# The first weight piece of two mixtures in four parts, and products nobody reads ahead of two waits of each router

## The reference

```python
def grouped_moe(h, router_w, router_b, w_gate, w_up, w_down):
    scores = jax.nn.sigmoid(t @ router_w)                # 16 experts
    sel = scores + router_b
    # best of 4 groups by the sum of its two best experts, then two experts in that group
    combine = ...                                        # (tokens, 16), mostly zero
    for e in range(N_EXPERTS):
        he = jax.nn.silu(t @ w_gate[e]) * (t @ w_up[e])
        y = y + combine[:, e:e + 1] * (he @ w_down[e])

def first_block(x, c, ...):
    for layer in range(2):
        mod = (silu(c) @ ada_w[layer] + ada_b[layer])    # six rows: shifts, scales, gates
        h = rms_norm(x, norm1_g[layer]) * (1.0 + sc1) + sh1
        x = x + g1 * (even_mixer(h, ...) if layer == 0 else odd_mixer(h, ...))
        h = rms_norm(x, norm2_g[layer]) * (1.0 + sc2) + sh2
        x = x + g2 * grouped_moe(h, ...)

def second_block(x, mem, ...):                           # after it, two more layers:
    # feed-forward, rwkv7 or dilated attention, each beside attention to mem, feed-forward
```

## Time and profile before

| | us |
|---|---|
| time, median of 3 runs | 2259.53 (2258.82 to 2261.78) |
| time of the profiled execution | 2259.21 |
| its span | 2257.4 |
| PE busy | 2159.8 (96%) |
| DVE busy | 1408.3 (62%) |
| ACT busy | 1030.3 (46%) |

### The profile page before, as it was taken

The page is one execution under the profiler, slowest core; times in us unless marked ns, Lnnn a source line. Parts: engine busy times, 40 slices in busy tenths (PEclk is TensorE's granted clock), DMA queues, the critical chain, the costliest instruction groups (busy, mean ns, idle before and its releaser), DMA issues.

```text
span 2257.4 us, 32929 instructions
## 1 busy us (share of the span) xinstructions
PE 2159.8 (96%) x14046; PEld 1774.0 (79%) x14046; DVE 1408.3 (62%) x1456; ACT 1030.3 (46%) x1155; POOL 80.8 (4%) x138
## 2 busy tenths in 40 slices
PE   6998899999999899999999999889999999999999
PEld 4777777678787777678788897778888888888887
DVE  5776745689775743499756555466566576635654
ACT  4344422367545423277544445335444444435443
POOL 2040000000000000000000000000000000020000
PEclk9999899999999899999999999999999999999999
DMA  9872869999670858999555550005554555433553
GB/s 345 308 250 96 305 244 368 367 345 368 207 255 1 282 188 314 333 339 364 196 188 186 186 168 18 4 34 197 198 187 167 184 182 203 146 88 126 192 186 112
DMA packets 267313, 475.61 MB, mean 211 GB/s; under 512 B 9424, under 2 KB 151824, under 8 KB 262944
## 3 DMA queue, kind: packets, MB, share of 16 engines
q1 hardware_dynamic: 256128, 431.81, 55.0%
q0 software_dynamic: 11040, 41.70, 5.4%
HBM read 471.33 MB, written 2.14 MB: 210 GB/s over the span
## 4 chain that ended last, share of the span: by engine, by line
PE 86%; DVE 6%; ACT 4%; DMA 2%; issue 1%; POOL 0%; ACTq 0%; DVEq 0%; SPq 0%; POOLq 0%
PE psum L1074 14%; PE psum L1076 7%; PE psum L1091 3%; PE psum L1093 3%; PE psum L1092 3%; PE psum L1042 3%; PE psum L1044 3%; PE psum L1043 3%; PE psum L1411 3%; PE psum L1366 2%; PE psum L1367 2%; PE psum L1368 2%; PE psum L1523 2%; PE psum L1525 2%; PE psum L1524 2%; DVE w_lo L2806 2%
## 5 line engine op out<-in xcount | busy, mean ns | idle before, releaser
L2806 DVE TENSOR_TENSOR w_lo<-ring,w_hi 128x2048 fp32r<-128x2048 f32 x267 | 609.9, 2289 | 288.3 <-ACT w_hi L2157 282.1
L2157 ACT ACTIVATE w_hi<-ring 128x2048 fp32r<-128x2048 f32 x267 | 510.8, 1915 | 367.9 <-PE psum L1093 119.8
L1074 PE MATMUL psum<-h_both,w_hi 128*128 128x512 f32 x1408 | 499.4, 399 | 1.6 <-DVE h_both L3500 1.3
L1076 PE MATMUL psum<-h_both,w_lo 128*128 128x256 f32 x1408 | 395.3, 281 | 0.0
L1074 PEld LDWEIGHTS psum<-h_both,w_hi 128*128 128x128 f32 x1408 | 264.5, 188 | 68.0 <-issue 1.7
L1076 PEld LDWEIGHTS psum<-h_both,w_lo 128*128 128x128 f32 x1408 | 265.9, 189 | 1.4
L2806 DVE TENSOR_TENSOR w_lo<-pool,w_hi 128x2048 fp32r<-128x2048 f32 x70 | 160.4, 2292 | 103.7 <-ACT w_hi L2157 103.3
L2157 ACT ACTIVATE w_hi<-pool 128x2048 fp32r<-128x2048 f32 x70 | 134.1, 1916 | 161.5 <-DMA pool<-in_exp_w_up 58.9
L2179 ACT ACTIVATE pool<-psum 128x512 f32<-128x512 f32 x88 | 52.6, 598 | 261.1 <-PE psum L1076 261.1
L1042 PE MATMUL psum<-w_hi,h_both 128*128 128x512 f32 (+1 forms) x352 | 142.1, 404 | 5.7 <-DVE w_lo L2806 2.7
L1366 PE MATMUL psum<-h_both,w_hi 128*128 128x256 f32 x480 | 139.1, 290 | 0.2 <-DVE w_lo L2806 0.2
(11 more groups left out here) (476 smaller groups left out, 3795.6 us busy)
## 6 DMA issues: line engine op xcount, KB each, us to landing
ring<-in_ffn_pre_w_in SPq DMA_DIRECT2D x44, 1024.0 KB, 5.1
ring<-in_ffn_post_w_in SPq DMA_DIRECT2D x44, 1024.0 KB, 5.1
pool<-in_exp_w_up SPq DMA_DIRECT2D x40, 1024.0 KB, 7.9
ring<-in_exp_w_gate SPq DMA_DIRECT2D x36, 1024.0 KB, 7.6
ring<-in_exp_w_down SPq DMA_DIRECT2D x30, 1024.0 KB, 7.6
ring<-in_ada_w SPq DMA_DIRECT2D x24, 1024.0 KB, 7.0
ring<-in_ffn_pre_w_out SPq DMA_DIRECT2D x22, 1024.0 KB, 4.8
ring<-in_ffn_post_w_out SPq DMA_DIRECT2D x22, 1024.0 KB, 4.9
```

Source lines behind the costliest of these rows:

```text
L1074: pe.matmul(o.rearrange("p (s n) -> p s n", s=2), wh[:, k, fs], h_both[:, :, k, :], start=k == 0, stop=False, skip_group_check=True)
L1076: m = pe.matmul(o[:, 0:T], wl[:, k, fs], h_hi[:, k, :], start=False, stop=k == KD - 1, skip_group_check=True)
L2157: act.activation(w_hi[:, (s["split"] + r) % 3, :], piece(s["pieces"][r]), ACT.Copy)\
L2806: dve.tensor_tensor(w_lo[:, slot, :], piece(s["pieces"][r]), w_hi[:, slot, :].bitcast(F32), ALU.subtract).then_inc(sem("w_lo"), 1)
```

## The change

First, the first piece of each mixture is loaded in four parts of 256 columns by two blocks, cast in four parts, and multiplied in high parts in four steps; DVE makes its low part in two halves. Second, the broadcast of the experts' weights is split: its first half stays in the router, its second stands behind the second quarter of the first piece; the copies of it move from the router into the mixture on ACT and DVE. Third, PE makes 5 (layer 0) or 10 (layer 1) unread products ahead of its wait for `group_picked` and 7 ahead of its wait for `comb_tok`. Fourth, the new semaphores `part_in0` to `part_in3` take the places of others: `mem_w01`, `cols_in` and `hot_in` become one, `tables_in`, and each wait for one of them becomes a wait for all ten loads (160); `rotated` and the first three quarters share `rotated_parts_hi`; `rwkv_in` and `stored` are counted on `landed0`.

```diff
+TABLES = 160
...
+                self.add(kind, (name, c, half), ("w_lo", self.split), slot, 0 if n == 0 else 1)
...
+                    elif n == m["first"]:
+                        src, dst = expert(kind, layer, 4 * group[0], 0), piece(n).rearrange("p (k n) -> p k n", k=KD)
+                        for j in range(4):
+                            sp.dma_start(dst[:, 2 * j:2 * j + 2, :], src[:, 2 * j:2 * j + 2, :]).then_inc(sem(f"part_in{j}"), 16)
...
-                pl.dma_start(mem_w[layer][half], src).then_inc(sem("mem_w1" if layer else f"mem_w0{half}"), 16)
+                pl.dma_start(mem_w[layer][half], src).then_inc(sem("mem_w1" if layer else ("tables_in" if half else "mem_w0")), 16)
...
-            pl.dma_start(rcols[:, :], a["rwkv_cols"]).then_inc(sem("cols_in"), 16)
+            pl.dma_start(rcols[:, :], a["rwkv_cols"]).then_inc(sem("tables_in"), 16)
             pl.dma_start(gains64[:, :, :], a["gains64"].partition_broadcast(P).rearrange("p (n d) -> p n d", d=64))\
-              .then_inc(sem("cols_in"), 16)
-            pl.dma_start(router_b[:, :], a["router_b"].partition_broadcast(P)).then_inc(sem("cols_in"), 16)
-            pl.dma_start(router_w[:, :, :], a["router_w"].rearrange("(k p) n -> p k n", p=P)).then_inc(sem("cols_in"), 16)
...
+              .then_inc(sem("tables_in"), 16)
+            pl.dma_start(router_b[:, :], a["router_b"].partition_broadcast(P)).then_inc(sem("tables_in"), 16)
+            pl.dma_start(router_w[:, :, :], a["router_w"].rearrange("(k p) n -> p k n", p=P)).then_inc(sem("tables_in"), 16)
...
-            pl.dma_start(view(WORK + 4240, 12)[0:32, :], a["rel_bias_2"]).then_inc(sem("hot_in"), 16)
...
+            pl.dma_start(view(WORK + 4240, 12)[0:32, :], a["rel_bias_2"]).then_inc(sem("tables_in"), 16)
...
-                    pe.wait_ge(sem("cols_in"), 64)
-                    pe.wait_ge(sem("hot_in"), 80)
+                    pe.wait_ge(sem("tables_in"), TABLES)
...
-            pe.wait_ge(sem("mem_w01"), 16)
+            pe.wait_ge(sem("tables_in"), TABLES)
             mem_products(0, 4)
             pe.wait_ge(sem("ada_used"), KD)
...
+                warm(10 if layer else 5, 2)
                 pe.wait_ge(sem("group_picked"), layer + 1)
                 picked = rt[:, 392:400]
                 pe.matmul(bank(6)[:, 0:8], K["ones"], picked, start=True, stop=True).then_inc(sem("group_sums"), 1)
                 pe.matmul(bank(7)[:, 0:8], K["ones"], picked, start=True, stop=False)
                 pe.matmul(bank(7)[:, 0:8], K["neg_from"], picked, start=False, stop=True).then_inc(sem("group_sums"), 1)
+                warm(7, 2)
                 pe.wait_ge(sem("comb_tok"), layer + 1)
                 for t in range(NT):
                     m = pe.transpose(bank(5)[0:NE, P * t:P * t + P], comb_tok[:, NE * t:NE * t + NE], ident)
                 m.then_inc(sem("comb_T_ps"), 1)
                 pe.wait_ge(sem("comb_T"), layer + 1)
                 pe.wait_ge(sem("places_in"), layer + 1)
-                for e in range(4):
-                    m = pe.matmul(bank(6 + e // 2)[:, T * (e % 2):T * (e % 2) + T],
-                                  bc(ident[0:NE, e:e + 1], [NE, P]), comb_t, start=True, stop=True)
-                    if e % 2:
-                        m.then_inc(sem("comb_ps"), 1)
+                comb_rows(0)
+
+            def comb_rows(half):
+
+                for e in range(2):
+                    m = pe.matmul(bank(6 + half)[:, T * e:T * e + T], bc(ident[0:NE, 2 * half + e:2 * half + e + 1], [NE, P]), comb_t,
+                                  start=True, stop=True)
+                m.then_inc(sem("comb_ps"), 1)
 
...
                     n = at[kind, c, 0]
-                    if n == 0:
-                        pe.wait_ge(sem("w_split_hi"), U0 + 1)
-                    else:
+                    if n > 0:
                         pe.wait_ge(sem("w_lo"), U0 + n + 1)
                     pe.wait_ge(sem("silu_done" if kind == "gate" else "hid_ready"), G0 + c + 1)
                     wh, wl = halves(n, HC)
                     if n == 0:
-                        for f in range(2):
-                            for k in range(KD):
-                                o, fs = bank(4)[:, T * f:T * f + T], slice(P * f, P * f + P)
-                                pe.matmul(o, wh[:, k, fs], h_hi[:, k, :], start=k == 0 and f == 0, stop=False, skip_group_check=True)
-                                pe.matmul(o, wh[:, k, fs], h_lo[:, k, :], start=False, stop=False, skip_group_check=True)
+                        for j in range(4):
+                            if j < 3:
+                                pe.wait_ge(sem("rotated_parts_hi"), 1 + 3 * layer + j + 1)
+                            else:
+                                pe.wait_ge(sem("w_split_hi"), U0 + 1)
+                            for k in (2 * j, 2 * j + 1):
+                                for f in range(2):
+                                    o, fs = bank(4)[:, T * f:T * f + T], slice(P * f, P * f + P)
+                                    pe.matmul(o, wh[:, k, fs], h_hi[:, k, :], start=k == 0 and f == 0, stop=False, skip_group_check=True)
+                                    pe.matmul(o, wh[:, k, fs], h_lo[:, k, :], start=False, stop=False, skip_group_check=True)
+                            if j == 1:
+                                comb_rows(1)
                         pe.wait_ge(sem("w_lo"), U0 + 1)
...
-            pe.wait_ge(sem("rwkv_in"), 96)
+            pe.wait_ge(sem("landed0"), PL.rwkv_landed)
...
-            act.wait_ge(sem("cols_in"), 64)
+            act.wait_ge(sem("tables_in"), TABLES)
             split_piece("even_in", 0, 0)
...
-                act.wait_ge(sem("comb_ps"), 2 * layer + 1)
-                act.activation(flat(comb_b[:, 0:2, :]), bank(6), ACT.Copy).then_inc(sem("side_act"), 1)
...
-                for n in range(3):
+                act.wait_ge(sem("w_used"), U0 - 2)
+                for j in range(4):
+                    cols = slice(512 * j, 512 * j + 512)
+                    act.wait_ge(sem(f"part_in{j}"), 16 + 16 * layer)
+                    act.activation(w_hi[:, U0 % 3, cols], piece(m_["first"])[:, cols], ACT.Copy)\
+                       .then_inc(sem("rotated_parts_hi" if j < 3 else "w_split_hi"), 1)
+                    if j == 1:
+                        act.wait_ge(sem("comb_ps"), 2 * layer + 1)
+                        act.activation(flat(comb_b[:, 0:2, :]), bank(6), ACT.Copy).then_inc(sem("side_act"), 1)
+                for n in range(1, 3):
                     split(n)
...
-                    dve.memset(tiny[:, 160:161], 0.0).then_inc(sem("rotated"), 1)
+                    dve.memset(tiny[:, 160:161], 0.0).then_inc(sem("rotated_parts_hi"), 1)
...
-                dve.wait_ge(sem("comb_ps"), 2 * layer + 2)
-                dve.tensor_copy(flat(comb_b[:, 2:4, :]), bank(7)).then_inc(sem("side_dve"), 1)
...
-                for n in range(4):
+                for j in range(2):
+                    cols = slice(1024 * j, 1024 * j + 1024)
+                    if j == 0:
+                        dve.wait_ge(sem("rotated_parts_hi"), 1 + 3 * layer + 2)
+                    else:
+                        dve.wait_ge(sem("w_split_hi"), U0 + 1)
+                    m = dve.tensor_tensor(w_lo[:, U0 % 3, cols], piece(m_["first"])[:, cols], w_hi[:, U0 % 3, cols].bitcast(F32),
+                                          ALU.subtract)
+                m.then_inc(sem("w_lo"), 1)
+                dve.wait_ge(sem("comb_ps"), 2 * layer + 2)
+                dve.tensor_copy(flat(comb_b[:, 2:4, :]), bank(7)).then_inc(sem("side_dve"), 1)
+                for n in range(1, 4):
                     split(n)
-                    if n > 0:
-                        ada_parts(0, n - 1)
+                    ada_parts(0, n - 1)
                 product(0)
```

More of the change, by code:

```diff
@@ L162, in rwkv @@
         self.held[0] = self.held[1] = ("rwkv_over", 1)
+        self.loads[0] += 6
+        self.rwkv_landed = 16 * self.loads[0]
         self.slot = 2
@@ L233, in moe @@
                 self.split += 1
-                self.add(kind, (name, c, half), ("w_lo", self.split), slot)
+                self.add(kind, (name, c, half), ("w_lo", self.split), slot, 0 if n == 0 else 1)
         self.swi[name] = m
@@ L710, in static_piece @@
                         rows = rwkv_par[64:P] if m == 1 else rwkv_par[0:src.shape[0]]
-                        sp.dma_start(rows[:, o:o + src.shape[1]], src).then_inc(sem("rwkv_in"), 16)
+                        sp.dma_start(rows[:, o:o + src.shape[1]], src).then_inc(sem("landed0"), 16)
                 else:
@@ L756, in _ @@
             sp.wait_ge(sem("x_new"), 10)
-            sp.dma_start(out.rearrange("a (t p) d -> p (a t) d", p=P), x[:, :, :]).then_inc(sem("stored"), 16)
-            sp.wait_ge(sem("stored"), 16)
+            sp.dma_start(out.rearrange("a (t p) d -> p (a t) d", p=P), x[:, :, :]).then_inc(sem("landed0"), 16)
+            sp.wait_ge(sem("landed0"), 16 * PL.loads[0] + 16)
```

(21 more changed lines are left out.)

4 lines of the change are left out of this document (removed).

## The result

The kernel after takes 2270.95 us (median of 6 runs, 2266.93 to 2275.33), the kernel before 2260.08 (6 runs beside it, 2258.82 to 2261.78): a ratio of 1.0048, 95% interval 1.0035 to 1.0061, thus 7.9 to 13.8 us slower. The forecast was 2266.0 in 2261 to 2271: the sign is right, the size 5 us short. The profiled execution of after is the fastest of the six, 2266.93, with a span of 2265.0; that is 7.7 above the profiled execution of before (2259.21) and within 1 us of the forecast, so the trace shows the causes of 7.7 us, and some 3 of the median's 10.9 lie outside it. Two executions of the kernel before in the sets measured later took 4212 and 9146 us; they count as slow and are left out everywhere.

A forecast was written before the change was run, and what follows sets the result against it. PE was taken to bound the kernel (2159.8 of 2257.4 us busy). From 2259.2, the start's +6.7 and the two mixtures' 0.0 gave 2265.9, say 2266 us, with 2261 to 2271 for 8 in 10.

The forecast's parts named there:

- The start, +6.7: Fifth memory product waits for the last of ten loads: 5.0 us hole plus 1.7 low clock, bounds 3.2 to 8.6.
- the two low stretches: At the start, clock at 0.50 under four memory records (+1.7 us), and again after the narrow products (already paid before).
- Rival (1): At the start, the tables land in time, PE does not wait and only the mixtures count: 2259 us; 10%.
- The unread products, +1.1 and +2.3: In the routers, products ahead of `group_picked` overrun their gaps, delaying group sums 1.1 us in layer 0, 2.3 in layer 1.
- The seven ahead of `comb_tok`: In the router, seven unread products take 3.0 us; 0.5 falls on `comb_T`, hidden behind the load.
- So the issues keep ahead and the whole lands when it did.: First piece's four loads: issues 0.5 us apart, a quarter moves in 0.75, so splitting delays no landing.
- The estimate beside it: Mixture loads, from the skill: 2.0 us per 256 KB, 8.0 for four; second piece 1.8 later per layer, 2270 in the end.
- The steps' worth, -2.0 and -2.2: In the mixtures, an earlier first piece gains at most PE's lateness for the second: 2.0 us layer 0, 2.2 layer 1.
- The copy moved on DVE: In the mixture, only up to 0.6 us for a copy of `comb_b` between casts was counted; second piece's low part unchanged.
- Cold holes, +0.8: In PE's 2 to 3 us holes before each second piece, the clock may fall: 0.4 us each, bounds 0 and 1.7.
- The sum: Whole kernel: 2259.2 + 6.7 for the start + 0.0 for the two mixtures = 2265.9, say 2266 us.
- Rival (4): In the routers, unread products run at half clock to their end, 3.1 and 5.5 late: 2270, with cold holes 2274; 15%.

The follow-up runs named there:

- e1: Kernel before with only the start's merge, all ten loads counted on `tables_in` and each wait for the whole: ratio 1.0037, +8.4 us.
- e7: Kernel before with only the unread products added ahead of the two waits of each router: ratio 1.0014, +3.2 us.
- e8: Kernel before with only the first piece's load in four, cast as a whole after all four: ratio 1.0005, +1.1 us.
- e5: Kernel after with PE's fifth memory product waiting for its own load, one load, no unread products, broadcast and copies back in the router: ratio 0.9997 to before.
- e9: Kernel before with only the first piece's casts in four, four product steps and low part in halves, on one load: ratio 0.9997, -0.7 us.
- e3: Kernel after with PE's fifth memory product waiting for its own load and the first piece in one load: 2271.54 us, ratio 1.0045 to before.
- e6: e3 with the broadcast's second half and both copies back in the router, unread products left: 2266.62 us, ratio 1.0024 to before.

## Why the prediction was right in sign and short in size

- **The start, +6.7.** Right: 6.85 in the profile, by the two low stretches that it named; in other executions more (e1: 10.7), +8.4 in the time. Rival (1) falls.
- **The unread products, +1.1 and +2.3.** Right in the mean for layer 1, too high for layer 0: +0.4 and +2.3 over the profiles, +3.2 (0.5 to 5.9) in e7's time. In the profile of after layer 0 had none, since the clock was still full there, and in layer 1 SP's first issue was 0.8 later. The seven ahead of `comb_tok` were hidden, as said.
- **"So the issues keep ahead and the whole lands when it did."** This step failed. The quarters moved at 269 GB/s instead of 344; the fourth came 2.1 later and the second piece 1.9. With that PE waited for the second piece's low part in both layers, 1.93 and 1.54 us, and of the -2.0 and -2.2 of the steps 0.0 and -0.8 were left. In time the split is not shown: +1.1 in e8, with an interval from -1.6 to +3.8. The estimate beside it, from the Trainium skill (DMA: Bandwidth & Descriptors, "Bandwidth"), was 1.8 per mixture; the 24 measured starts give 1.8. Its table is for loads issued from GpSimd and has no 256 KB, so that the figures meet so closely is partly luck. I had set it aside because no row showed a quarter, and should have given it a chance of its own, with 2270.
- **The steps' worth, -2.0 and -2.2.** This is the term that was mis-sized most, and the late quarters are not all of it: with one load that landed on time, e5 and e9 give -0.7 in time (e9: -2.7 to +1.4), not -4.2, and in the rows -0.5 to -0.7 in layer 0 and -1.4 in layer 1. The prediction took the whole of a cap ("at most what PE was late") as its value. PE gets to the first piece earlier, but at half clock, where the head start shrinks: in e9 it was low until 242.8 for a piece begun at 239.0, and in e5 and e9 PE still came 0.9 to 1.3 behind the low part.
- **The copy moved on DVE.** The prediction saw ACT's copy between the quarters and not DVE's ahead of the second low part. It cost nothing in after, hidden by the late load; in e3 the low part started 1.9 and 2.1 later for it than in e6, and the time, with the broadcast and ACT's copy moved too, was 4.7 us longer.
- **Cold holes, +0.8.** The clock was full in both holes and behind them. It was low for 3.4 us inside each first piece instead (245.0 to 248.4 and 763.8 to 767.2), as it had been before; no run separates what that costs.
- **The sum.** With -2.0 and -2.2 replaced by 0 the terms give 2259.2 + 6.7 + 1.1 + 2.3 + 0.8 = 2270.1, beside a median of 2270.95. That it fits so well is partly luck: in the profile layer 0's own term was zero and layer 1's 0.8, which with the steps' 0.0 and -0.8 gives 0.0 for both mixtures, the very sum that was forecast from other terms; the profiled execution, 2266.93, is where the forecast put it. The median lies 4.0 above that execution, and e1's start, +8.4, is larger than mine. Rival (4) gave 2270 as well, but by its own mechanism (both layers' unread products at half clock) it did not happen: layer 0's ran at full clock.

On the clock the prediction set the Trainium skill (TensorE: Matmul & The Clock Gate, "What's actually happening") aside as disagreeing with the rows. The router of after, at 1.00 from 235 to 244 with PE busy 7.89 of 9 us, against 0.50 with 4.32 of 9 before, agrees with its rule that activity keeps the clock up. Behind the narrow products at the start it fell all the same, with PE busy in the records throughout.

What stays open: how much of the 10.9 us each part has to within 2 us, and why four quarters move more slowly than one load. Start, unread products, four loads and steps measured alone add up to 8.4 + 3.2 + 1.1 - 0.7 = 12.0, and each has an interval of 2 us or more to either side.

## What to carry to other kernels

Semaphores that are merged to save numbers make every waiter wait for the slowest load; look at each of them, and behind the first at the next, which it hides. Splitting a load pays only if the parts and what is queued behind them land as early as the whole did; here the second load came 1.9 us later for it, about what the earlier start gave. What an engine is late by is the most that a head start can win, not what it will win: here a quarter to two thirds of it. Work moved out of one engine's row lands in another's: check what stands behind it in that row. And an unread product in front of a wait is free only if it ends before the wait does: five did in layer 0 while the clock was full, ten in layer 1 never did.

## What was not expected

The spread over executions of one kernel, 6 to 14 us, goes with PE's clock: over the 29 to 34 executions of the kernel before in each set, time and mean granted clock have a correlation of about -0.8. The same router of layer 0 cost up to 2.8 us more with no instruction changed, and the same start 6.85 or 10.7. One profiled execution gives a term of this kernel to about 3 us. Six runs of the kernel before lay within 3 us of each other; the 29 to 34 of each later set did not.
